# The group norm of the RWKV heads moved into the chunk recurrence, its output gate computed as a weight stage, the merge gates fetched into chunks already read, and splits that cover only a unit's rows

## The chip, the cores and the metric

The kernel runs on one core of a Trainium2 chip. The metric is the device time of one execution in microseconds (us). The kernel before takes 3714.7 us (median of three runs, 3714.55 to 3715.57).

## The reference

The program is a five layer model over 512 tokens of width 1024, in float32. The first four layers (two RG-LRU mixers, a gated spatial mixer, a short convolution, each with an MLP) are touched by the change in one detail only. The fifth layer is where the change sits:

```
rw = shifted projections;  q, k, v, gate_r, gate_a = the rest of n @ w_in
g = sigmoid(p_gd) @ g2                                  # 160 x 1024
y = rwkv7_scan(r, decay, k, v, -kk, kk * a)             # 16 heads of 64, token by token
mean, var over the 64 channels of a head
yn = (y - mean) * rsqrt(var + GN_EPS) * gn_w + gn_b
y_rwkv = (yn + sum(r * k * r_k) * v) * g
merged = sigmoid(gate_r) * (y_rwkv @ p_rwkv) + sigmoid(gate_a) * (y_attn @ p_attn)
h = h + merged @ w_out, then cross attention and an MLP
```

`sum(r * k * r_k) * v` is called the bonus.

## The kernel before, in words

**Layout and weight stages.** Activations lie with channels on the 128 partitions and the 512 tokens along the free axis, so a tensor of width 1024 is 8 tiles of 128x512. Nearly all dense products go through a weight stage. A stage consists of groups, each giving two output tiles, and a group of one or two units. A unit is a block of kb x 128 weight rows by 256 columns. SyncE loads it into one of two slots of `raw` (`sp_stage`, L374), ScalarE copies it to the rounded `wh` (L387), VectorE computes the rest `wl = raw - wh` (L391), and TensorE multiplies three terms (xh*wh, xl*wh, xh*wl, L441) for each 128 rows and each output tile: 6 matmuls for each k, 48 for a unit of 8, 30 for one of 5 (`l0_out` and `l3_out`, two units a group), 12 for one of 2 (`p_attn`). Both copies work on all 8 row blocks of the slot, whatever kb is. The next unit's split stands in each engine's queue ahead of the work on this group's results (`split_next`, L394). Evacuated activations are split in the same way (`act_upper` L776 gives yh, `dve_lower_y` L780 gives yl).

**Order of the fifth layer.** The queues of the engines are written out by hand, in program order: ... `rkv`, `gates2`, then `pe_chunks`, `pe_heads`, the stage `merge`, `out2`. The sigmoids of the 16 merge gate tiles go to DRAM (`gate_spill`) from `tmp` (L1200), the 8 bonus tiles as well (L1449).

**Chunks (L1542 to L1693).** The recurrence runs over 8 chunks of 64 tokens. In a chunk, five levels (l = 1 to 5) of small 64x64 products invert a triangular matrix: `Y` (L1559), then `X` (L1578) and `Z` (L1579), where ScalarE copies Y out and VectorE adds X and Z. W0 is made in levels 2 and 3, then come U (L1586), the new state (L1593, L1595) and the chunk's output (L1599 to L1603), which ScalarE copies into `VT` (L1635). The halves of the partitions (`HP`) hold two heads, and their products alternate. TensorE turns V, B and K of the next chunk by an identity (`i64`, L1534).

**Heads (L1696 to L1757).** After the last chunk GpSimd fetches g2 and the bonus. For each of the 8 tiles TensorE sums over heads (L1702), VectorE centres (L1738), ScalarE squares (L1721), TensorE sums again (L1712), ScalarE takes the root (L1725), VectorE takes the reciprocal of 128x512 (L1747), scales, adds the bonus and multiplies with the gate tile that TensorE made in float32 (L1715, L1716; L1748 to L1752). Splits of the result follow.

**Merge (L1781).** Eight groups alternate between p_rwkv (8 row blocks) and p_attn (2). GpSimd loads all gates with one 4 MB DMA (L1773) and then `x` (L1775).

Of the kernel before, what the change touches and what calls it, by code (L numbers as in the profile page):

```python
# [90 lines left out]
def build(nc, a, out):  # L91
# [39 lines left out]
    i64 = pers("i64", [P, CH])  # L131
    ARENA = used[0] + (WH_AT - used[0]) % 512
# [78 lines left out]
    gl = at("gl", 0, [P, 16, T], base_at=XH_AT)  # L211
    mg = at("mg", 0, [P, ND, T])
    g2s = at("g2s", 0, [P, 2, D])
    gns = at("gns", 8, [P, 3, T])
    bon = at("bon", 14, [P, 2, T])
# [21 lines left out]
    bonus_spill = nc.dram_tensor("bonus_spill", [ND, P, T], F32).ap()  # L237
    kv_spill = nc.dram_tensor("kv_spill", [P, 16, MEM], F32).ap()
# [27 lines left out]
    def stage(name, *args, **kw):  # L266
# [4 lines left out]
        back = {"x": ND, "h": 16, "y": 5 * st.upg if st.upg == 2 else ND + 2 * (name == "merge"), "m": None}[st.rhs]  # L271
# [4 lines left out]
        st.loop = st.kind in ("relu", "resid", "fin", "gelu", "sigm", "scale", "gelusq") and not st.classes  # L276
# [74 lines left out]
    tiles_split("ysplit", ND + 2)  # L351
# [18 lines left out]
    srcs = {"x": (xh, xl), "h": (hh, hl), "y": (yh, yl), "m": (mh, ml)}  # L370
# [3 lines left out]
    def sp_stage(sp, st):  # L374
        def body(p, first):
            for su in range(st.upg):
                w, r, kb, c = weights(st, p.j, su)
                src = w.rearrange("(k p) n -> p k n", p=P)[:, r:r + kb, bass.ds(c, 256)]
                sp.wait_ge(lower, p.unit(su) + 1)
                sp.dma_start(raw[:, p.slot(su), 0:kb], src).then_inc(landed[p.slot(su)], 16)  # L380
        run_groups(sp, st, body)

    def act_split(act, p, su):
# [16 lines left out]
    def pe_stage(pe, st):  # L400
        ops = srcs[st.rhs]
        need = (lambda k: st.need0 + k + 1) if st.need0 is not None else None

        def body(p, first):
            banks = [ps[2 * p.pair()], ps[2 * p.pair() + 1]]
            pe.wait_ge(evac, p.group() * 2 + 2)
            for su in range(st.upg):
                slot = p.slot(su)
                kb = st.kb if st.kind != "merge" else (8, 2)[p.c % 2]
# [17 lines left out]
                for k in range(kb):  # L427
                    kk = k0 + k
                    if st.kind == "merge" and p.c % 2:
                        kk = ND + k  # L430
                    if need and (p.c < 1 or st.kind == "merge"):
                        pe.wait_ge(split, need(kk))
# [6 lines left out]
                    for mt in mts:  # L439
                        for n_, (wt, oi) in enumerate(terms):  # L440
                            last = nc.tensor.matmul(banks[mt][:, 0:st.n], wt[:, slot, k, mt * P:mt * P + P],  # L441
                                                    ops[oi][:, kk, 0:st.n],
# [48 lines left out]
    def act_stage(act, st, dest=None, fn=None, custom=None):  # L491
        def body(p, first):
# [9 lines left out]
            for mt in range(2):  # L502
                t = p.j * 2 + mt
                if custom or st.kind in ("scale", "resid", "conv4", "tok", "memk", "memv"):
# [58 lines left out]
    def dve_stage(dve, st, dest=None, custom=None, early=None):  # L563
        def body(p, first):
            split_next(dve_split, dve, p, st)
            if first:
                dve_norm(dve, st.norm)
                if st.name == "q":
                    dve.wait_ge(s("mid_root"), 1)
                    nc.vector.reciprocal(acc1[:], acc1[:]).then_inc(s("mid_inverted"), 1)  # L570
# [108 lines left out]
    def pe_init(pe):  # L679
# [5 lines left out]
        last.then_inc(s("rows_turned"), 1)  # L685
# [23 lines left out]
    def dve_init(dve):  # L709
        dve.wait_ge(s("rows_turned"), 1)  # L710
# [5 lines left out]
        nc.vector.tensor_scalar(prm[1][:, G_SQ:G_SQ + ND], prm[1][:, G_SQ:G_SQ + ND], EPS, None, ALU.add).then_inc(s("mid_gains"), 1)  # L716
        nc.vector.tensor_scalar(omu[:, 0:27], prm[3][:, MU:MU + 27], -1.0, 1.0, ALU.mult, ALU.add)
        for t in range(ND):
            dve.wait_ge(s("x_turned"), t + 1)
# [5 lines left out]
    def act_init(act):  # L725
# [4 lines left out]
        act.wait_ge(s("mid_gains"), 1)  # L730
# [3 lines left out]
    def dve_softplus(dve):  # L734
# [21 lines left out]
        nc.vector.tensor_copy(small[:, 4:5], q[:, 0:1]).then_inc(s("c8_ready"), 1)  # L756
# [79 lines left out]
    def act_a(act, l):  # L836

        n, j = f"l{l}", l // 3
        for t0 in range(0, NR, 2):
# [5 lines left out]
            if t0 == 0:  # L845
                act.wait_ge(s("c8_ready"), 1)
# [171 lines left out]
    def pool_dist(pool):  # L1018


        pool.wait_ge(s("dist_free"), 1)
# [22 lines left out]
    def dve_x(dve, ts):  # L1044

        dve.wait_ge(s("mid_inverted"), 1)
# [1172 lines left out]
```

## Time and profile before

| | |
|---|---|
| median of three runs | 3714.7 us |
| the profiled execution's own time | 3715.44 us |
| its span in the profile | 3713.7 us |
| mean granted TensorE clock | 0.974 |
| TensorE busy, share of the span | 3553.9 us, 96% |
| VectorE busy | 1871.4 us, 50% |
| ScalarE busy | 1162.3 us, 31% |
| GpSimd busy | 442.4 us, 12% |

Busy time says how long an engine had an instruction in flight. Matmuls overlap (a 128x512 matmul counts 0.39 us and the next one starts 0.23 us later), so the share of TensorE tells of gaps, not of peak speed. The granted clock is the share of TensorE's full 2.4 GHz; 0.5 is its lower level, 1.2 GHz.

### The profile page before, as it was taken

Reading aid. Unit: us, or ns where it says so; the run is one execution under the profiler, and the core shown is the slowest. Engines: PE = TensorE matmul, PEld = TensorE weight load, DVE = VectorE, ACT = ScalarE, POOL = GpSimd, SP = SyncE. Lnnn points to the kernel's source line nnn. Section 1 sums busy time; section 2 is a strip of 40 time slices with the busy share of each in tenths; the row PEclk is TensorE's granted clock in tenths of the full one; section 3 lists DMA queues with packets and bytes.
Section 4 is the critical chain, followed back from the end, with each engine's and each line's share of the span. In section 5 each row is a group of like instructions: output and inputs, shape, how many; then the busy total and the mean of one; then the engine's idle time right before and its main releaser. Section 6 shows DMA issues by size and latency. Waiting matters only on the chain. (4 is left out here: it accounts for less than half of the span.)

```text
span 3713.7 us, 52132 instructions
## 1 busy us (share of the span) xinstructions
PE 3553.9 (96%) x21576; PEld 2877.8 (77%) x21576; DVE 1871.4 (50%) x2099; ACT 1162.3 (31%) x1319; POOL 442.4 (12%) x416
## 2 busy tenths in 40 slices
PE   7999999899999999999999999999999988989998
PEld 5578888778888888887678888887769965768886
DVE  7655244335344553346654344564785556455242
ACT  3632123222222232222632133233652222233122
POOL 1111011011011020111111012000220000112011
PEclk9999999889999999999999999999999989999998
DMA  3123233213223233233123323342220004312331
GB/s 123 60 84 102 94 98 96 68 57 102 91 91 101 91 102 102 91 102 103 50 88 102 98 93 104 105 130 97 89 83 21 4 24 155 101 46 91 102 101 57
DMA packets 296102, 324.80 MB, mean 87 GB/s; under 512 B 5971, under 2 KB 287958, under 8 KB 295415
## 3 DMA queue, kind: packets, MB, share of 16 engines
q1 hardware_dynamic: 288439, 295.92, 25.0%
q0 software_dynamic: 5184, 22.15, 1.7%
q10 hardware_dynamic: 2304, 4.20, 0.3%
q8 instruction: 134, 2.20, 0.3%
q14 instruction: 41, 0.34, 0.0%
HBM read 309.66 MB, written 12.58 MB: 87 GB/s over the span
## 5 line engine op out<-in xcount | busy, mean ns | idle before, releaser
L441 PE MATMUL ps<-xh,wh 128*128 128x512 f32 x2424 | 960.4, 396 | 25.4 <-DVE wl L391 22.0
L441 PE MATMUL ps<-xh,wl 128*128 128x512 f32 x2424 | 947.2, 391 | 0.0
L441 PE MATMUL ps<-xl,wh 128*128 128x512 f32 x2424 | 947.1, 391 | 0.0
L391 DVE TENSOR_TENSOR wl<-raw,wh 128x2048 fp32r<-128x2048 f32 x283 | 656.2, 2319 | 449.2 <-ACT wh L387 448.7
L387 ACT ACTIVATE wh<-raw 128x2048 fp32r<-128x2048 f32 x283 | 540.4, 1910 | 693.3 <-PE ps L441 668.5
L441 PEld LDWEIGHTS ps<-xh,wh 128*128 128x128 f32 x2424 | 457.7, 189 | 135.4 <-issue 36.9
L441 PEld LDWEIGHTS ps<-xl,wh 128*128 128x128 f32 x2424 | 457.9, 189 | 99.7 <-issue 5.8
L441 PEld LDWEIGHTS ps<-xh,wl 128*128 128x128 f32 x2424 | 457.4, 189 | 96.4
L441 PE MATMUL ps<-hh,wh 128*128 128x512 f32 x1280 | 498.3, 389 | 1.1 <-DVE wl L391 0.9
L441 PE MATMUL ps<-hl,wh 128*128 128x512 f32 x1280 | 498.0, 389 | 0.0
L441 PE MATMUL ps<-hh,wl 128*128 128x512 f32 x1280 | 497.9, 389 | 0.0
L542 POOL TENSOR_TENSOR hf<-tmp 128x512 f32<-128x512 f32 x160 | 163.3, 1042 | 1132.4 <-DVE tmp L580 1132.4
L511 ACT ACTIVATE hh<-tmp 128x512 f32 (+1 forms) x160 | 98.0, 634 | 598.6 <-DVE tmp L580 598.6
L441 PEld LDWEIGHTS ps<-hh,wh 128*128 128x128 f32 x1280 | 240.3, 188 | 52.1 <-DVE wl L391 2.4
L441 PEld LDWEIGHTS ps<-hh,wl 128*128 128x128 f32 x1280 | 240.3, 188 | 50.1
L441 PEld LDWEIGHTS ps<-hl,wh 128*128 128x128 f32 x1280 | 240.3, 188 | 49.6
L580 DVE SCALAR_TENSOR_TENSOR tmp<-ps,rs 128x512 f32<-128x512 f32 x160 | 103.1, 686 | 341.1 <-PE ps L441 341.0
L591 DVE TENSOR_TENSOR x<-x,ps 128x512 f32 (+1 forms) x128 | 82.3, 684 | 379.9 <-PE ps L441 379.9
L555 POOL TENSOR_TENSOR acc<-acc,hf 128x512 f32<-128x512 f32 x88 | 130.3, 1481 | 1057.5 <-ACT hf L523 1026.6
L441 PE MATMUL ps<-yh,wh 128*128 128x512 f32 x496 | 199.3, 402 | 29.9 <-DVE wl L391 17.6
L441 PE MATMUL ps<-yl,wh 128*128 128x512 f32 x496 | 197.2, 398 | 0.0
L441 PE MATMUL ps<-yh,wl 128*128 128x512 f32 x496 | 196.9, 397 | 0.0
(390 smaller groups left out, 3593.8 us busy)
## 6 DMA issues: line engine op xcount, KB each, us to landing
raw<-in_mlp_w SPq DMA_DIRECT2D x128, 1024.0 KB, 5.4
raw<-in_ffn_w SPq DMA_DIRECT2D x32, 1024.0 KB, 5.4
raw<-in_w_in SPq DMA_DIRECT2D x31, 1024.0 KB, 5.3
raw<-in_a_w_in SPq DMA_DIRECT2D x20, 1024.0 KB, 5.1
raw<-in_c_w_in SPq DMA_DIRECT2D x12, 1024.0 KB, 5.2
raw<-in_a_w_out SPq DMA_DIRECT2D x16, 640.0 KB, 4.4
raw<-in_b_w_in SPq DMA_DIRECT2D x8, 1024.0 KB, 5.4
raw<-in_xa_wkv SPq DMA_DIRECT2D x8, 1024.0 KB, 5.5
```

The lines of the kernel that those rows point to most:

```text
L387: nc.scalar.activation(wh[:, p.slot(su)], raw[:, p.slot(su)], ACT.Copy).then_inc(upper, 1)
L391: nc.vector.tensor_tensor(wl[:, p.slot(su)], raw[:, p.slot(su)], wh[:, p.slot(su)], ALU.subtract).then_inc(lower, 1)
L441: last = nc.tensor.matmul(banks[mt][:, 0:st.n], wt[:, slot, k, mt * P:mt * P + P], ops[oi][:, kk, 0:st.n], start=k == 0 and su == 0 and n_ ...
L511: nc.scalar.activation(hh[:, bass.ds(t, 1)], tmp[:, mt:mt + 1, 0:T], ACT.Square).then_inc(acted, 1)
L542: nc.gpsimd.tensor_tensor(hf[:, mt], tmp[:, mt, 0:T], tmp[:, mt, 0:T], ALU.mult).then_inc(pooled, 1)
L555: nc.gpsimd.tensor_tensor(acc[:], acc[:], sq[:, mt], ALU.add).then_inc(pooled, 1)
L580: nc.vector.scalar_tensor_tensor(out=tmp[:, mt, 0:T], in0=ps[b + mt][:], scalar=0.0, in1=rs[:], op0=ALU.max, op1=ALU.mult).then_inc(evac, 1)
L591: nc.vector.tensor_tensor(xt, xt, ps[b + mt][:].rearrange("p (a n) -> p a n", a=1), ALU.add).then_inc(evac, 1)
```

## The change

- **Splits of a unit's rows only.** L387 and L391 work on `rows_of(unit)` row blocks (5 in `l0_out` and `l3_out`, 2 for `p_attn` and g2), and stages with kb = 5 are no longer hardware loops.
- **Gate as a stage.** A new stage `g2` of four units (128 + 32 rows, 12 matmuls each) stands between `gates2` and the chunks. gd and the attention output ya are split for it and for the merge (`gdh`, `gdl`, `yah`, `yal`). Its tiles are copied to two holding places and stored in `g_spill`.
- **Norm in the recurrence.** V is turned by `c64` = identity - 1/64, so the chunk outputs are centred already. During chunk c+1 the norm of chunk c is done: squares (ScalarE), sums (8 matmuls, 2 columns each), root of 64x16, reciprocal of 64x16, 16 matmuls that spread the result, one multiply (VectorE), and three operations on GpSimd (gn_w, bonus + gn_b, gate). Bonus and gate slices come from DRAM into the read slices of B and K.
- **Merge.** The four p_attn groups come first, then the four of p_rwkv. Gates are fetched two tiles at a time into the chunk slices that were read.
- Some semaphores share a name now; no wait is changed by that.

```diff
-        st.loop = st.kind in ("relu", "resid", "fin", "gelu", "sigm", "scale", "gelusq") and not st.classes
+        st.loop = st.kind in ("relu", "resid", "fin", "gelu", "sigm", "scale", "gelusq") and not st.classes and st.kb != 5
+    stage("g2", a["g2_2"][0], 4, 1, 2, lin(0), rhs="g", kind="g2")
-            return (a["p_rwkv_2"][0], 0, 8, j // 2 * 256) if j % 2 == 0 else (a["p_attn_2"][0], 0, 2, j // 2 * 256)
+            return (a["p_attn_2"][0], 0, 2, j * 256) if j < 4 else (a["p_rwkv_2"][0], 0, 8, (j - 4) * 256)
...
+                if st.kind == "merge" and p.c == 1:
+                    sp_g(sp)
+                    sp_slices(sp)
...
-        nc.scalar.activation(wh[:, p.slot(su)], raw[:, p.slot(su)], ACT.Copy).then_inc(upper, 1)
+        nc.scalar.activation(wh[:, p.slot(su), 0:n], raw[:, p.slot(su), 0:n], ACT.Copy).then_inc(upper, 1)
-        nc.vector.tensor_tensor(wl[:, p.slot(su)], raw[:, p.slot(su)], wh[:, p.slot(su)],
+        nc.vector.tensor_tensor(wl[:, p.slot(su), 0:n], raw[:, p.slot(su), 0:n], wh[:, p.slot(su), 0:n],
...
+    def dve_g2(p, b):
+        if p.c < 2:
+            for mt in range(2):
+                nc.vector.wait_ge(s(f"gate_stored{mt}"), 128)
+        else:
+            nc.vector.wait_ge(s(f"g_stored{p.c % 2}"), 32)
+        for mt in range(2):
+            nc.vector.tensor_copy(G_HOLD[p.c % 2][mt], ps[b + mt][:]).then_inc(evac, 1)
+        if p.c == 0:
+            for h in range(2):
+                nc.vector.wait_ge(s("side_upper"), h + 3)
+                nc.vector.tensor_tensor(yal[:, h], ya[:, h], yah[:, h], ALU.subtract).then_inc(s("side_split"), 1)
+    def sp_g(sp):
+        for j in range(4):
+            for mt in range(2):
+                sp.wait_ge(evac, (stages["g2"].g0 + j) * 2 + 5 + mt)
+                sp.dma_start(g_spill[2 * j + mt], G_HOLD[j % 2][mt]).then_inc(s(f"g_stored{j % 2}"), 16)
+    def sp_slices(sp):
...
+        for c in range(NC):
+            sp.wait_ge(s("ck_turned"), 3 * c + 3)
+            if c:
+                sp.wait_ge(s("slices"), 32 * c)
+            tok = slice(c * CH, c * CH + CH)
+            sp.dma_start(BT[:, c], bonus_spill.rearrange("q p t -> p q t")[:, :, tok]).then_inc(s("slices"), 16)
+            sp.dma_start(KT[:, c], g_spill.rearrange("q p t -> p q t")[:, :, tok]).then_inc(s("slices"), 16)
...
+                    plink(nc.gpsimd.tensor_scalar(PT[e % 2][4], PT[e % 2][4], col(3, GNB + e), None, ALU.add))
...
+    def pe_head_sums(pe, c):
+        pe.wait_ge(s("hd_squared"), c + 1)
+        for q in range(NH2):
+            last = mm(ps[HB(c)][0:64, 2 * q:2 * q + 2], hs[c][:, q], headones[:, 0:P:64], start=True, stop=True)
+        last.then_inc(s("hd_sums"), 1)
+    def pe_head_spread(pe, c):
+        pe.wait_ge(s("hd_inverse"), c + 1)
+        for q in range(NH2):
+            for e in range(2):
+                last = mm(ps[HB(c)][HP[e], cols(q)], RT[:, 2 * q + e:2 * q + e + 1].to_broadcast([64, CH]), i64[0:64, :],
+                          start=True, stop=True)
+        last.then_inc(s("hd_spread"), 1)
...
@@ pe_chunks, levels
+                    if l == 2 and c:
+                        pe_head_sums(pe, c - 1)
+                if l == 5 and c:
+                    pe.wait_ge(s("ck_w0_copied"), 2 * c + 2)
+                    pe_head_spread(pe, c - 1)
...
@@ end of pe_chunks
         pe.wait_ge(s("ck_state"), NC)
+        pe_head_sums(pe, NC - 1)
+        pe_head_spread(pe, NC - 1)
...
@@ act_chunks, levels
+                if l == 1 and c:
+                    act_head_squares(act, c - 1)
+                if l == 2 and c:
+                    act_head_root(act, c - 1)
...
@@ dve_chunks
+                if l == 3 and c:
+                    dve_head_inverse(dve, c - 1)
+            if c:
+                dve_head_scale(dve, c - 1)
...
     def pool_heads(pool):
+        for c in range(NC):
+            tok = VT[:, :, c * CH:c * CH + CH]
+            pool.wait_ge(s("hd_scaled"), c + 1)
+            pool.wait_ge(s("slices"), 32 * c + 32)
+            plink(nc.gpsimd.tensor_tensor(hs[c][:], hs[c][:], prm[3][:, GNW:GNW + ND].unsqueeze(2).to_broadcast([P, NH2, CH]), ALU.mult))
+            plink(nc.gpsimd.tensor_tensor(hs[c][:], hs[c][:], BT[:, c], ALU.add))
+            nc.gpsimd.tensor_tensor(tok, hs[c][:], KT[:, c], ALU.mult).then_inc(s("ysplit_y"), 1)
...
+            pool.dma_start(gl[:, 2 * c:2 * c + 2], gate_spill[src:src + 2].rearrange("t p n -> p t n"))\
+                .then_inc(s("gates_back_attn" if c < 4 else "gates_back_rwkv"), 16)
...
@@ merge
+    def dve_before_merge(p):
+        if p.j == 3:
+            for t in range(2):
+                dve_lower_y(nc.vector, "ysplit", t, VT[:, t])
+    def act_merge(p):
+        ts = {2: (0, 1), 3: range(2, ND)}.get(p.j, ())
+        for t in ts:
+            act_upper(nc.scalar, "ysplit", t, VT[:, t], src=NC)
```

## Rows read from the trace of the kernel before

**Rows 1.** Timeline of TensorE: start us, duration, instructions, idle time ahead and its releaser.

```profile
214.58 0.80 PE L441 MATMUL ps<-yh,wh 128*128 128x512 f32 x1 [5.21 <-DVE wl L391]
...
232.17 0.50 PE L441 MATMUL ps<-yh,wh 128*128 128x512 f32 x1 [1.14 <-DVE wl L391]
...
2786.22 3.68 PE L1539 MATMUL ps<-AR,BT 64*64 64x128 f32 x32 [7.19 <-DVE small L1645]
...
3026.70 0.28 PE L1603 MATMUL ps<-TLK,cVt 64*64 64x64 f32 x4
...
3090.84 0.80 PE L441 MATMUL ps<-yh,wh 128*128 128x512 f32 x1
...
3158.00 0.77 PE L441 MATMUL ps<-yh,wh 128*128 128x512 f32 x1 [5.02 <-DVE yl L780]
3158.56 0.63 PE L441 MATMUL ps<-yl,wh 128*128 128x512 f32 x1
3158.99 0.63 PE L441 MATMUL ps<-yh,wl 128*128 128x512 f32 x1
```

**Rows 2.** Windows: stretch, length, busy PE, PEld, DVE, ACT, POOL, clock, DMA share, GB/s.

```profile
2786.20:3027.00 240.80, 237.10 (x7168) 229.20 (x7168) 126.95 (x270) 61.55 (x143) 0.15 (x1) 0.99 0.03 9
...
3033.60:3092.00 58.40, 47.35 (x67) 15.33 (x68) 51.52 (x45) 15.43 (x24) 4.94 (x8) 0.73 0.26 82
```

**Rows 3.** VectorE's groups by form, 2200 to 3300 us: busy, mean ns, idle.

```profile
L391 DVE TENSOR_TENSOR wl<-raw,wh 128x2048 fp32r<-128x2048 f32 x63 | 145.7, 2313 | 100.1 <-ACT wh L387 100.1
...
L1747 DVE RECIPROCAL gns<-gns 128x512 f32<-128x512 f32 x8 | 26.8, 3348 | 2.9 <-ACT gns L1725 2.9
...
L1924 DVE COPY qx<-ps 128x512 f32<-128x512 f32 x8 | 5.2, 686 | 20.1 <-PE ps L1899 20.1
```

**Rows 4.** DMA issues: KB each, median us from issue to landing.

```profile
gate_spill<-tmp ACTq DMA_DIRECT2D x16, 256.0 KB, 2.0
raw<-in_p_rwkv SPq DMA_DIRECT2D x4, 1024.0 KB, 5.3
...
x<-x_spill POOLq DMA_DIRECT2D x1, 2048.0 KB, 19.4
```

**Rows 5.** Timelines of ScalarE and VectorE in a chunk: waits after level 1 and level 5.

```profile
2918.50 0.38 ACT L1627 ACTIVATE cYt<-ps 128x256 f32<-128x256 f32 x1 [2.18 <-PE ps L1559]
...
2903.56 1.29 DVE L1651 TENSOR_TENSOR TLB<-ps,acc 128x512 f32<-128x512 f32 x2 [1.33 <-PE ps L1539]
```

**Rows 6.** GpSimd's groups by form.

```profile
L1443 POOL TENSOR_TENSOR KT<-rt 128x512 f32<-128x512 f32 x8 | 10.4, 1297 | 0.0
```

**Rows 7.** Timeline of TensorE in a chunk: level 4 and the start of level 5.

```profile
2925.82 1.37 PE L1559 MATMUL ps<-cX,cTM 64*64 64x64 f32 x32
2927.03 0.63 PE L1578 MATMUL ps<-cYt,cZ 64*64 64x64 f32 x16
...
2928.89 1.37 PE L1559 MATMUL ps<-cX,cTM 64*64 64x64 f32 x32
```

**Rows 8.** Timeline of TensorE around eight tiny matmuls between two weight units.

```profile
2314.27 0.39 PE L441 MATMUL ps<-xl,wh 128*128 128x512 f32 x1
2314.50 0.39 PE L441 MATMUL ps<-xh,wl 128*128 128x512 f32 x1
2314.82 1.05 PE L1064 MATMUL ps<-ones,rs 1*128 1x1 f32 x8
2315.79 0.50 PE L441 MATMUL ps<-xh,wh 128*128 128x512 f32 x1
```

**Rows 9.** Timeline of TensorE in an attention slot: float32, 64 rows, 128 moving columns.

```profile
2493.55 0.38 PE L1097 MATMUL ps<-kT,qT 64*128 64x128 f32 x2
2493.77 0.38 PE L1098 MATMUL ps<-kT,qT 64*128 64x128 f32 x2
```

**Rows 10.** Timelines of ScalarE and VectorE in `l0_out`, ahead of its fourth unit.

```profile
227.74 1.91 ACT L387 ACTIVATE wh<-raw 128x2048 fp32r<-128x2048 f32 x1
...
229.67 2.44 DVE L391 TENSOR_TENSOR wl<-raw,wh 128x2048 fp32r<-128x2048 f32 x1 [0.86 <-ACT wh L387]
```

More of the change, by code:

```diff
@@ L210, in build @@
     tgtf = at("tgtf", 1.25, [P, CH], base_at=XT_AT)
[L211 to L215, printed above, removed]
+    gl = at("gl", 0, [P, 16, T])
+    mg = at("mg", 0, [P, ND, T], base_at=XH_AT)
+    hs = [at(f"hs{c}", 4 * c, [P, NH2, CH]) for c in range(NC)]
+    gdh = at("gdh", 2, [P, 2, T], F32R, base_at=XT_AT)
+    gdl = at("gdl", 84, [P, 2, T], F32R)
+    yah = at("yah", 28, [P, 2, T], F32R, base_at=XH_AT)
+    yal = at("yal", 80, [P, 2, T], F32R)
     qx = at("qx", 0, [P, ND, T])
@@ L366, in weights, with rows_of @@
         if st.kind == "merge":
-            return (a["p_rwkv_2"][0], 0, 8, j // 2 * 256) if j % 2 == 0 else (a["p_attn_2"][0], 0, 2, j // 2 * 256)
+            return (a["p_attn_2"][0], 0, 2, j * 256) if j < 4 else (a["p_rwkv_2"][0], 0, 8, (j - 4) * 256)
         return st.w, st.row0 + su * st.kb, st.kb, st.col(j)
-    srcs = {"x": (xh, xl), "h": (hh, hl), "y": (yh, yl), "m": (mh, ml)}
+    srcs = {"x": (xh, xl), "h": (hh, hl), "y": (yh, yl), "m": (mh, ml), "g": (gdh, gdl)}
+    unit_rows = [8 if st.kind != "merge" and st.kb is None else st.kb if st.kb else (2 if c < 4 else 8)
+                 for st in order for c in range(st.groups) for _ in range(st.upg)]
+    G2_U0 = stages["g2"].u0
+    def rows_of(u):
+        return unit_rows[u] if isinstance(u, int) else 8
     def sp_stage(sp, st):
@@ L684, in pe_init @@
                                        ident[0:n_rows[i], 0:n_rows[i]])
[L685 removed]
+        last.then_inc(s("x_turned"), 1)
         pe.wait_ge(s("x_landed"), 16)
@@ L1200, in act_gates @@
             act.dma_start(gate_spill[p.st.first + t], tmp[:, mt, 0:T]).then_inc(s(f"gate_stored{mt}"), 16)
+        if p.st.name == "gates2" and p.c == 0:
+            act.wait_ge(s("pair_pooled"), 5 * ND - 5)
+            act.wait_ge(s("lora_ready"), 3)
+            for h in range(2):
+                act.activation(gdh[:, h], gd[:, h], ACT.Copy).then_inc(s("side_upper"), 1)
         act_attn_slot(act, k)
@@ L1212, in dve_gates, with act_g2 @@
                 dve_chunk_masks(nc.vector)
+                for h in range(2):
+                    nc.vector.wait_ge(s("side_upper"), h + 1)
+                    nc.vector.tensor_tensor(gdl[:, h], gd[:, h], gdh[:, h], ALU.subtract).then_inc(s("side_split"), 1)
         dve_attn_scores(nc.vector, after_group(p.st, p.c))
+    G_HOLD = [[tmp[:, 0, 0:T], tmp[:, 1, 0:T]], [rs[:], rt[:, 0]]]
+    def dve_g2(p, b):
[6 more added lines that the diff above has]
+            nc.vector.tensor_copy(G_HOLD[p.c % 2][mt], ps[b + mt][:]).then_inc(evac, 1)
+        if p.c == 0:
+            for h in range(2):
+                nc.vector.wait_ge(s("side_upper"), h + 3)
+                nc.vector.tensor_tensor(yal[:, h], ya[:, h], yah[:, h], ALU.subtract).then_inc(s("side_split"), 1)
+    def act_g2(p):
+        if p.c == 0:
+            nc.scalar.wait_ge(units, stages["gates2"].u0 + 4)
+            for h in range(2):
+                nc.scalar.activation(yah[:, h], ya[:, h], ACT.Copy).then_inc(s("side_upper"), 1)
+    def sp_g(sp):
[4 more added lines that the diff above has]
+    def sp_slices(sp):
+        for m in range(2):
+            sp.wait_ge(s(f"bonus_stored{m}"), 64)
+            sp.wait_ge(s(f"g_stored{m}"), 64)
+        for c in range(NC):
[5 more added lines that the diff above has]
+            sp.dma_start(KT[:, c], g_spill.rearrange("q p t -> p q t")[:, :, tok]).then_inc(s("slices"), 16)
     def shift_scale(p, mts, mu, dests):
@@ L1718, in act_heads @@
-    def act_heads(act):
-        def root(q):
-            act.wait_ge(s("hd_centred"), q + 1)
-            act.activation(gns[:, 2], VT[:, q], ACT.Square).then_inc(s("hd_squared"), 1)
-            act.wait_ge(s("hd_var"), q + 1)
-            if q >= 2:
-                act.wait_ge(s("ysplit_y"), q - 1)
-            act.activation(gns[:, q % 2], ps[5][:], ACT.Sqrt, scale=1.0 / 64, bias=small[:, 1:2]).then_inc(s("hd_root"), 1)
-        root(0)
-        for q in range(ND):
-            if q + 1 < ND:
-                root(q + 1)
-            act_upper(act, "ysplit", q, VT[:, q])
-        for h in range(2):
-            act.activation(yh[:, ND + h], ya[:, h], ACT.Copy).then_inc(acted, 1)
@@ L1825, in act_mem_norm @@
             act.wait_ge(s("mem_summed"), c + 1)
-        act.activation(msq[:, 2:4], msq[:, 0:2], ACT.Sqrt, scale=1.0 / D, bias=small[:, 0:1]).then_inc(s("mem_root"), 1)
+        act.activation(msq[:, 2:4], msq[:, 0:2], ACT.Sqrt, scale=1.0 / D, bias=small[:, 0:1]).then_inc(s("mem_summed"), 1)
     MEM_TILES = (0, 2, 4, 6, 1, 3, 5, 7)
```

180 lines of the change are left out of this document (91 added, 89 removed).

## The prediction

> **What bounds the kernel now.** I read the page first: TensorE is in flight 96% of the span (the table above), so only two things can move the time, its own work and its gaps. Then I listed the gaps from its timeline [rows 1]: between the end of `gates2` and the start of `out2` stands the largest cluster of the kernel, and `l0_out` and `l3_out` show four each that end with a weight split (5.21 us once, and then three like the one of 1.14). The windows [rows 2] say what each stretch is made of. In the chunks (240.8 us) TensorE is busy 237.1 us at a granted clock of 0.99: that stage is bound by TensorE. In the heads stage VectorE is busy 51.5 of 58.4 us, and TensorE's clock is 0.73: that stage is bound by VectorE, above all by eight reciprocals of 3.35 us [rows 3]. The merge is bound by TensorE again.
>
> The stations of TensorE before, from [rows 1]: `gates2` ends at 2786.2 - 7.2 = 2779.0; the chunks run from 2786.2 to 3027.0; the merge starts at 3090.8; `out2` starts at 3158.0. I predict the last station, then add `l0_out` and `l3_out`.
>
> **The g2 stage, up to the chunks.** On TensorE it is 4 x 12 matmuls, 0.227 us apart when the clock is up (the pair that shows it stands further down), 10.9 us. VectorE, which today is late already (it releases the chunks 7.2 us after TensorE is free), gets more: 8 copies of PSUM by 0.686 [rows 3] = 5.5; four subtractions for gd and ya, of the same 512 columns and as long, 2.7; five splits of 2 row blocks by some 0.7 in place of one of 2.3, +1.2; one small operation, 0.2. That is 9.6. To this come waits that the new order makes: the first copy needs the last gate tile stored (2.0 us after its issue [rows 4]), and the third needs the first g tiles stored, whose DMA stands in SyncE's queue behind the load of merge unit 0, which waits for the split of g2 unit 2. Followed instruction by instruction, the copies of group 2 start at about 2794.3, those of group 3 at 2796.7, and the chunks at 2798.9: **+12.7 us**. Bounds: 8.5 (VectorE's work less what it waits through today) and 18 (each of the two holding places waits a store and its queue in full).
>
> **In the chunks, seven times.** ScalarE's squares (some 0.6) fall behind its Y copies of level 1, where it then waits 2.2 us; root and reciprocal are 64x16 and small; VectorE's multiply (0.69) falls into 1.3 us that it waits for the B products [rows 5]; GpSimd's three operations (1.3 each [rows 6], some 4.5 with their links) have a chunk of 29 us. If these covers were gone, a chunk would be 0.6 to 0.7 us longer for each. TensorE has no cover: a level is 96 instructions in 3.07 us, 2.80 us of them issue at 29 ns [rows 7], so what is added to it lies on the path. A float32 matmul is two instructions. Sums: 16 instructions, each with 64 weight columns and 2 moving. The nearest rows are eight instructions with 128 weight columns and one moving, 0.97 us, 0.12 each [rows 8]; half the columns give some 0.06, so 1.0 us. Leaving the 64x64 pattern and coming back costs some: that same break starts 0.09 us later than the pitch would have it [rows 8]; I take 0.3 with the semaphore. Bounds 0.5 (29 ns each) and 1.9 (0.12 each). Spread: 32 instructions, 64 weight columns, 64 moving. All read the lower 64 partitions, so they can't alternate between halves as the pairs at 29 ns do. Two instructions with 64 rows and 128 moving columns take 0.22 us [rows 9], 0.11 each, so 64 columns take 0.055: 1.7 us. Bounds 0.9 (as pairs) and 3.4 (0.107 each, load and multiply one after the other). The spread stands where TensorE waits 0.25 us for the last Y copy, which it fills. Sum 1.3 + 1.7 - 0.25 = 2.75, times seven **+19.3 us** (8 to 36).
>
> The Trainium skill says (TensorE: Matmul & The Clock Gate, The mechanism) that a weight load overlaps a running matmul only when the row group differs. By that rule the spread would cost 3.4 us and the sum 12 us more. The trace disagrees where it can be seen: matmuls that all use the full array, each with its own weights, start 0.227 us apart, which is little more than 512 columns take [rows 8], and the instructions of [rows 9], all on the same 64 rows, come no slower than their moving columns ask for.
>
> **After the chunks.** Let T be the end of the last chunk, 2798.9 + 240.8 + 19.3 = 3059.0. The last norm has no cover: output copy and squares until T+1.5, sums T+2.8, root and reciprocal T+3.9, spread T+6.0 or somewhat more at the lower clock. The merge starts at T+6.5, where before it started 63.8 us after the chunks: **-57.3 us**. The heads stage is gone, since the reciprocals of 512 columns became ones of 16 and the rest went to GpSimd.
>
> **Merge to out2.** The matmuls are the same 240, 54.4 us. Before, the stretch took 67.2 us, with gaps for a split of 2.3 us behind an evacuation between the units, and 5.0 at its end [rows 1]. Now the four short units come first. They finish by T+19.5, and the first p_rwkv unit is late: its load waits for the split of p_attn unit 2 (T+11.5), takes 5.3 us alone [rows 4] and more beside the gates and `x` (2 MB), which GpSimd issues at about T+13, so it lands at T+18.5; ScalarE +1.9, VectorE +2.3, the lower part of y tile 0 +0.7: TensorE starts at T+23.7, with a clock that has to come up (1.9 us: after 5 us of idling, nine matmuls stood 0.43 apart, not 0.227 [rows 1]). Four units of 10.9 us then run without a gap, to T+69.2. The next stage's split is no longer in front of the last evacuation, so `out2` starts 2.8 + 0.7 us later, T+72.5. From merge start that is 66.0: **-1.2 us**. GpSimd's last three operations (done by T+12.5) hide behind the short units. If that cover were gone, `out2` would move with them.
>
> Sum of the layer: 12.7 + 19.3 - 57.3 - 1.2 = **-26.5 us**; `out2` starts at 3131.5.
>
> **Splits of five row blocks.** In `l0_out` the fourth unit's split runs 1.91 on ScalarE and 2.44 on VectorE, one after the other behind the evacuation, and TensorE waits 1.14 for it [rows 1, 10]. With 5/8 of the columns they take 1.2 and 1.45, 1.7 us less in all, so the gap goes. The first matmul behind the gap is 0.1 to 0.2 us longer too, so I take 1.3 for each. The first gap (5.21) shrinks by ScalarE 0.7 and VectorE 0.85, 1.5. 1.5 + 3 x 1.3 = 5.4 for each stage, **-11 us** for both. Bounds: 8 (the first gap stays) and 13 (it shrinks by the whole 1.7 and the clock comes up sooner). Splits of other stages are untouched.
>
> Total -37.5, against the profiled execution's own 3715.4 (0.7 above the median): 3677.9, or **3677 us** beside the median.
>
> **Rivals.**
> 1. The spread's loads are not hidden. For it: nothing in this kernel alternates two column halves over the same 64 rows. Against: [rows 9]. Worth 1.7 x 7 = 12: 3689 us. It is what the rule of the Trainium skill above would give.
> 2. The transfers crowd: gates, `x` and the weights of two p_rwkv units meet at T+13, and `x` took 19.4 us beside the 4 MB gate load [rows 4]. Each us that unit lands later is a us; with the g2 stage at its upper bound too (stores waited in full), 3 to 10 us: 3684.
> 3. Cheaper small work: sums and spread issue at 29 ns as the pairs do, and g2 is at its lower bound. 19.3 becomes 8, 12.7 becomes 9: 3662 us.
> 4. Row splits don't bite, because another queue holds those units (the activation's own split, ScalarE's wait for the multiply before). Then -3 in place of -11: 3685.
> 5. Slower than before. Sums are a full-height pattern in a stream of 64x64 ones, and every change of pattern might drain the array. There are 14 changes, two for each of seven chunks; they undo the gain of 37.5 us only above 2.7 us each, and then 3715 and beyond. Against: the break in [rows 8] starts 0.09 us late. The Trainium skill (TensorEngine Tiling (Array Packing), Key Properties) does say that switching the tiling mode drains TensorE, but gives no price; [rows 8] show one that is small.
>
> **How the numbers follow.** Forecast 0.50, with its own range 3668 to 3686; rival 1 0.15; rival 2 0.12; rival 3 0.12; rival 4 0.04; rival 5 0.04 for its full form and 0.03 for a weak one that ends within 0.2% of no change. 0.2% is 7.4 us, about what a measurement of this kernel can tell from no change. Faster 0.93, same 0.03, slower 0.04. The range that leaves out no more than 2 in 10 reaches from the middle of rival 3 and its half above, 3661, to beyond rival 1, 3696.
>
> **What would show it.** In the profile after: the first chunk product 20 us after `gates2`; 27 to 28 us of further chunk time against 240.8 would speak for rival 1, 19 for the forecast, 8 for rival 3; the clock in the chunks stays at 0.99; no reciprocal of 128x512 after the chunks; one gap of some 4 us before the first p_rwkv unit and none between units; periods of 13.6 us in `l0_out`. It would be wrong if the chunk levels start to wait on ScalarE or VectorE, or if the clock falls in the chunks.

## The result, and the profile after

The changed kernel takes 3677.8 us (median of 4 runs, 3676.4 to 3684.7), the one before 3714.8 us; the ratio is 0.990, 95% interval 0.989 to 0.992. The prediction was 3677 us. The profiled execution's own time is 3676.4 us, its span 3674.2 us.

Timeline of TensorE of the changed kernel at its stations (columns as in [rows 1]):

```profile
211.97 0.79 PE L476 MATMUL ps<-yh,wh 128*128 128x512 f32 x1 [3.77 <-DVE wl L417]
...
2768.29 0.76 PE L476 MATMUL ps<-gdh,wh 128*128 128x512 f32 x1 [4.45 <-DVE wl L417]
...
2784.76 3.61 PE L1625 MATMUL ps<-AR,BT 64*64 64x128 f32 x32 [2.19 <-DVE small L1786]
...
3040.67 0.28 PE L1735 MATMUL ps<-TLK,cVt 64*64 64x64 f32 x4
3042.59 1.06 PE L1637 MATMUL ps<-headones,hs 128*64 128x2 f32 x16 [1.63 <-DVE cST L1838]
3044.29 1.97 PE L1645 MATMUL ps<-i,small 64*64 64x64 f32 x32 [0.64 <-DVE small L1659]
3046.20 0.79 PE L476 MATMUL ps<-yah,wh 128*128 128x512 f32 x1
...
3068.84 0.77 PE L476 MATMUL ps<-yh,wh 128*128 128x512 f32 x1 [9.21 <-DVE yl L815]
...
3119.01 0.54 PE L476 MATMUL ps<-yh,wh 128*128 128x512 f32 x1 [3.53 <-DVE yl L815]
```

Against [rows 1]: `gates2` ends at 2763.8 (idle time of 4.45 ahead of 2768.29), where it ended at 2779.0. The chunks follow 20.9 us later instead of 7.2. The last chunk ends at 3041.0 (its last row starts at 3040.67). The merge starts 5.2 us after that instead of 63.8. Of the four idle times in `l0_out`, the first fell from 5.21 to 3.77 and the three of 1.14 are gone. A gap of 9.2 us stands ahead of the first p_rwkv unit, and none between units.

Windows of the changed kernel: g2, chunks, last norm, p_attn groups, the gap, p_rwkv groups (columns as in [rows 2]).

```profile
2763.80:2784.80 21.00, 14.17 (x51) 9.11 (x50) 15.84 (x32) 4.72 (x8) 2.15 (x2) 0.92 0.41 150
2784.80:3041.00 256.20, 250.79 (x7504) 242.76 (x7504) 139.22 (x284) 68.34 (x158) 32.28 (x28) 0.99 0.14 36
3041.00:3046.20 5.20, 2.97 (x49) 2.80 (x49) 1.62 (x3) 2.02 (x4) 0.00 (x0) 0.80 0.29 99
3046.20:3059.60 13.40, 13.40 (x50) 10.55 (x48) 6.35 (x10) 2.31 (x4) 5.28 (x5) 0.82 0.57 209
3059.60:3068.80 9.20, 0.03 (x1) 0.00 (x0) 3.00 (x3) 4.95 (x8) 0.00 (x0) 0.77 0.71 237
3068.80:3119.00 50.20, 46.64 (x192) 38.04 (x193) 25.55 (x31) 11.13 (x12) 0.44 (x1) 0.94 0.32 105
```

The chunk stage has 336 instructions more (7 x 48) and is 15.4 us longer than in [rows 2]. TensorE is still busy for nearly all of it, with the clock at 0.99. In the gap TensorE has nothing, the DMA engines are at 0.71, and 237 GB/s is the highest rate of these windows. That what TensorE waits for there is a transfer is shown by ScalarE's row under runs 3 and 4.

Timeline of VectorE of the changed kernel in the g2 stage, at its longest wait:

```profile
2780.95 1.29 DVE L1269 COPY tmp<-ps 128x512 f32<-128x512 f32 x2 [3.02 <-DMA g_spill<-tmp]
```

The copy of g2's third group waits 3.0 us for the first g tiles to be stored, which is the wait that the prediction put there.

Timeline of TensorE in the chunk that [rows 5] and [rows 7] show: sums in level 2, and the spread of the chunk before.

```profile
2904.44 1.04 PE L1645 MATMUL ps<-i,small 64*64 64x64 f32 x30
2905.27 0.27 PE L1709 MATMUL ps<-cZ,cYt 64*64 64x64 f32 x1
2905.32 0.22 PE L1645 MATMUL ps<-i,small 64*64 64x64 f32 x1
2905.37 1.04 PE L1709 MATMUL ps<-cZ,cYt 64*64 64x64 f32 x30
...
2925.41 1.09 PE L1637 MATMUL ps<-headones,hs 128*64 128x2 f32 x16
2926.43 0.68 PE L1708 MATMUL ps<-cYt,cZ 64*64 64x64 f32 x16
```

The x30 of the spread start at 2904.44 and the next product's x30 at 2905.37: 32 instructions in 0.93 us, 29 ns each, the pitch of the pairs in [rows 7]. The 16 of the sums take 1.02, 64 ns each.

The chunks are not all alike. From its first product to that of the next, each of the second to the seventh takes 29.66 to 29.83 us in the kernel before. In the changed kernel three of them take 31.47 to 31.59 and the other three 32.09 to 32.34. In the long ones TensorE stops for a moment in the middle of a level, and the profile names no engine for it:

```profile
2891.86 0.50 PE L1682 MATMUL ps<-cX,cTM 64*64 64x64 f32 x9 [0.54 <-issue]
```

There are four such breaks, 1.4 us in all. The kernel before has none.

### The profile page after: what moved, and what is told of

The parts are those of the page before. It is cut to its first block and busy times, and to the rows that moved or that the text cites. A ratio compares the mean times of both kernels' runs of the same rounds, so it can differ in the third digit from the quotient of the medians.

```text
span 3674.2 us, 52665 instructions
## 1 busy us (share of the span) xinstructions
PE 3536.7 (96%) x21944; PEld 2888.8 (79%) x21944; DVE 1827.8 (50%) x2090; ACT 1145.6 (31%) x1325; POOL 490.6 (13%) x445
## 5 line engine op out<-in xcount | busy, mean ns | idle before, releaser
L417 DVE TENSOR_TENSOR wl<-raw,wh 128x2048 fp32r<-128x2048 f32 (+2 forms) x287 | 642.6, 2240 | 457.4 <-ACT wh L412 456.8
L412 ACT ACTIVATE wh<-raw 128x2048 fp32r<-128x2048 f32 (+2 forms) x287 | 527.1, 1837 | 712.3 <-PE ps L476 678.2
L476 PE MATMUL ps<-yh,wh 128*128 128x512 f32 x480 | 192.0, 400 | 22.4 <-DVE yl L815 12.7
```

The lines of the kernel that those rows point to most:

```text
L412: nc.scalar.activation(wh[:, p.slot(su), 0:n], raw[:, p.slot(su), 0:n], ACT.Copy).then_inc(upper, 1)
L417: nc.vector.tensor_tensor(wl[:, p.slot(su), 0:n], raw[:, p.slot(su), 0:n], wh[:, p.slot(su), 0:n], ALU.subtract).then_inc(lower, 1)
L476: last = nc.tensor.matmul(banks[mt][:, 0:st.n], wt[at_, slot, k, mt * P:mt * P + P], ops[oi][at_, kk, 0:st.n], start=k == 0 and su == 0 an ...
```

## The experiments

Each was timed beside the kernel before (3714.6 to 3715.9 us). Medians are of 4 executions where nothing else is said. Single executions of one kernel scatter by up to 11 us here (run 7), so each verdict goes by the median and by the stations of the trace together. T is the end of the last chunk, and "after T" counts from there. For each run the diff shows its main lines; "..." stands for lines left out.

**1. Rows undone.** The changed kernel, with eight row blocks split in `l0_out` and `l3_out`.

```diff
-        return unit_rows[u] if isinstance(u, int) else 8
+        return unit_rows[u] if isinstance(u, int) and unit_rows[u] != 5 else 8
```

> The changed kernel with one part undone: the splits of the two stages with five row blocks (l0_out and l3_out) work on all eight row blocks again; these stages stay written out and everything else stays as changed. From the two traces, the changed kernel's TensorE is 6.6 us ahead before the end of layer 0 and 15.2 us ahead at the end of gates2. If the shorter splits made all of that, this kernel takes 3677.8 + 15 = 3693 us. If my working holds (5.4 us a stage) and the rest comes from elsewhere, 3689. Rival: writing the loops out instead of running them as hardware loops made the gain, not the rows; then this kernel stays at 3678 to 3682, and the gaps before the fourth and later units of l0_out stay closed.

Measured: 3685.3 us, 7.5 above the changed kernel. That fits neither theory and not the rival in full: part of the gain stays with eight row blocks.

**2. Loops out, in the kernel before.** The other half: only the loop flag of the change.

```diff
-... "gelusq") and not st.classes
+... "gelusq") and not st.classes and st.kb != 5
```

> The kernel before with one line of the change alone: the stages with five row blocks (l0_out, l3_out) are written out instead of running as hardware loops; the splits still work on eight row blocks. In the run with the rows undone and the loops out, the gaps before the later units of l0_out were 0.57 us where the kernel before has 1.14, and the units came 14.5 us apart instead of 15.0 to 15.1; its TensorE was 5.8 us ahead of the kernel before at g2, where the changed kernel is 15.2 ahead. Theory: writing the loops out is worth 5 to 6 us by itself, 3709.3; the rows are the other 9.4. Rival: the loops cost nothing, the 5.8 us came from elsewhere in the change (semaphores that share a name, placement), and this kernel stays at 3714.8.

Measured: 3708.2 us (10 executions, 3706.2 to 3710.7), 6.5 less than before; ratio 0.998 (0.997 to 0.999, which is 3 to 10 us). Timeline of TensorE in `l0_out` of this kernel:

```profile
229.96 0.50 PE L441 MATMUL ps<-yh,wh 128*128 128x512 f32 x1 [0.58 <-DVE wl L391]
...
244.42 0.50 PE L441 MATMUL ps<-yh,wh 128*128 128x512 f32 x1 [0.56 <-DVE wl L391]
```

The groups come 14.46 us apart, and each gap is half of the 1.14 of [rows 1]; the trace still names the split as what ended it. So of each gap half was the hardware loop's and half the split's. From the first product of `l0_out` to the first of the next stage, and the same for `l3_out`, TensorE takes 133.8 us in the kernel before, 129.0 in this one and 122.4 in the changed one. So in the traces the loops are worth 4.8 us (3.8 of it in the six gaps) and the rows 6.6, together 11.4 for both stages. The medians say 6.5 and 7.5; the traces don't show the difference in these stages.

**3 and 4. Transfers held.** In run 3 GpSimd's load of x waits until ScalarE has split the first p_rwkv unit. In run 4 the last gates and the second p_rwkv load wait for that too (the second and third piece below).

```diff
         pool.wait_ge(s("x_stored"), 16)
+        pool.wait_ge(upper, stages["merge"].u0 + 5)
         pool.dma_start(x[:], x_spill)
...
+            if c == NC - 1:
+                pool.wait_ge(upper, stages["merge"].u0 + 5)
             pool.wait_ge(s("ysplit_y"), c + 1)
...
+                if st.kind == "merge" and p.c == 5:
+                    sp.wait_ge(upper, p.unit(su))
```

> The changed kernel with one transfer moved: GpSimd issues the 2 MB load of x only after ScalarE has split the first p_rwkv unit. Theory (transfers crowd): the first p_rwkv load took 10.4 us instead of 5.3 because x, issued 1.1 us before it, shares the DMA engines; a quarter MB of gates and the second p_rwkv load still share. I expect a landing 6.5 us after the issue, the gap before the first p_rwkv unit 9.2 - 4 = 5.2 us, and 3674 us. Rival: the time is that of SyncE's own queue, where the loads of units 4 and 5 share the engines; then the gap stays at 9 us and the time at 3678. A second way to fail: x is then late for the last stage of the layer and out2 waits for it.

> As the run before, and two more transfers are held: the last pair of gates (0.5 MB) also waits until the first p_rwkv unit is split, and SyncE's load of the second p_rwkv unit waits until then too. The first p_rwkv load then has the engines for itself. Theory (transfers crowd): landing 5.3 us after the issue as in the kernel before, gap 4.1 us, out2 5 us earlier than in the changed kernel, 3673 us. Against the run before it tells what the second load and the gates cost: 1.2 us by this theory, nothing if x alone was the crowd. Rival: the load is slow by itself here (gap stays 9 us, 3678).

Measured: 3675.6 and 3670.6 us, 2.2 and 7.2 below the changed kernel. Timelines of SyncE's queue and ScalarE: changed kernel, x later, all held, in this order.

```profile
3053.38 15.10 SPq L401 DMA_DIRECT2D raw<-in_p_rwkv  x3
...
3063.85 1.91 ACT L412 ACTIVATE wh<-raw 128x2048 fp32r<-128x2048 f32 x1 [7.90 <-DMA raw<-in_p_rwkv]
```

```profile
3060.01 11.96 SPq L401 DMA_DIRECT2D raw<-in_p_rwkv  x3
...
3067.34 1.91 ACT L412 ACTIVATE wh<-raw 128x2048 fp32r<-128x2048 f32 x1 [4.79 <-DMA raw<-in_p_rwkv]
```

```profile
3061.27 9.56 SPq L403 DMA_DIRECT2D raw<-in_p_rwkv  x3
...
3066.20 1.92 ACT L414 ACTIVATE wh<-raw 128x2048 fp32r<-128x2048 f32 x1 [2.36 <-DMA raw<-in_p_rwkv]
...
3071.18 0.47 PE L478 MATMUL ps<-yh,wh 128*128 128x512 f32 x1 [3.68 <-DVE yl L817]
```

From issue to the split's start it is 10.5, 7.3 and 4.9 us, and the gap is 9.2, 6.1 and 3.7 us. The load is slowed by all that runs beside it: x is worth 3 us of the gap, gates and second load together 2.4. `out2` starts 78.0, 74.4 and 69.8 us after T. Holding x cost nothing later: from `out2` to the end it is 555 us in all three. Both profiled executions are the slowest of their four; ahead of T, the stretch from `gates2` to the chunks took 4.8 and 7.2 us longer in them than in the changed kernel (see runs 11 and 12).

**5. Spread twice.** In the seven covered chunks.

```diff
-        for q in range(NH2):
+        for q in list(range(NH2)) * (2 if c < NC - 1 else 1):
             for e in range(2):
```

> The changed kernel in which TensorE computes the spread of the head norm twice (same values into the same bank) in each of the seven chunks that run under the next one: 32 more instructions a chunk. If they cost 29 ns each, as the row of the changed kernel says (x30 in 0.9 us), the seven add 6.5 us: 3684.3. By my forecast's price (0.055 us each) 12.3 us: 3690. If a weight load waits for the running matmul of the same 64 rows (0.107 us each), 24 us: 3702. The second copy has no wait to fill, so this is the bare price.

Measured: 3681.7 us, 3.9 more. The stretch from the first to the last chunk is 6.3 us longer, 0.9 us a chunk for 32 instructions, 28 ns each. This settles the price: rows 7, not rows 9.

**6. Sums in two places.**

```diff
+                if l == 2 and c:
+                    pe.wait_ge(s("ck_out"), c)
+                    pe_head_sums(pe, c - 1, range(0, 4))
...
-                        pe_head_sums(pe, c - 1)
+                        pe_head_sums(pe, c - 1, range(4, NH2))
```

> The changed kernel with the eight head sums of a chunk in two places, four before and four after the first W0 products of level 2, in the seven chunks that run under the next one: the same instructions, but two more changes of pattern (64x64 to full height and back) in each of seven chunks. If a change of pattern costs what the changed kernel's rows show (some 0.1 to 0.2 us a break), the time rises by 1 us, within what a measurement can tell. If changes of pattern drain the array at more than 2.7 us each, as rival 5 had it, it rises by 38 us. The first half also has to wait for ScalarE's squares one place earlier; 0.5 us a chunk if they are late.

Measured: 3683.1 us (one execution 3676.2). In the trace the chunks start 6.7 us later than in the changed kernel, where the two are alike; 4.8 of that is the g2 stage, with the clock at 0.66. The chunks themselves are 0.8 us longer. Their breaks without a releaser are shorter here (0.8 us in all, not 1.4), so without them the difference is 1.4 us, some 0.1 us for each of the 14 more changes of pattern. Chunks without a break say the same: 31.7 to 31.8 us instead of 31.5. A change of pattern has a price, but it is far from rival 5's 2.7 us.

**7. GpSimd's work out.** One column in place of the three operations, in seven chunks.

```diff
+            if c < NC - 1:
+                nc.gpsimd.tensor_tensor(VT[:, 0, c * CH:c * CH + 1], hs[c][:, 0, 0:1], KT[:, c, 0, 0:1], ALU.mult).then_inc(s("ysplit_y"), 1)
+            else:
...
```

> Leaves out: GpSimd's three operations (gn_w, bonus, gate) of the first seven chunks, for each of which one single-column product stands; the last chunk is whole. It prices what GpSimd's work costs the recurrence that it lies under. In the changed kernel two of VectorE's operations on SBUF took 0.98 and 1.71 us for the pair instead of 0.69 and 0.76 while GpSimd worked, and TensorE shows a new gap of 0.39 us behind them. Theory: contention costs 0.4 us a chunk, 3675 us. Rival: TensorE is the bound of the chunk and hides it, 3678 us (no change). A third: the rest of the added chunk time (2.2 us a chunk, of which sums and spread are 2.0) is all matmuls, which says the same as the rival.

Measured: 3680.6 us (3674.6 to 3685.5), the chunks as long as in the changed kernel (within 0.1 us). VectorE's groups in the chunks, of the changed kernel and of this one (columns as in [rows 3]):

```profile
L1807 DVE TENSOR_TENSOR cZ<-cTM,i 128x256 f32<-128x256 f32 x16 | 11.8, 776 | 0.3
...
L1803 DVE TENSOR_TENSOR cTM<-TLB,acc 128x512 f32<-128x512 f32 x8 | 7.2, 906 | 0.3
```

```profile
L1807 DVE TENSOR_TENSOR cZ<-cTM,i 128x256 f32<-128x256 f32 x16 | 6.1, 422 | 0.3
...
L1803 DVE TENSOR_TENSOR cTM<-TLB,acc 128x512 f32<-128x512 f32 x8 | 5.5, 692 | 0.3
```

The contention is real, 7.4 us of VectorE's time in all, and hidden: VectorE waits later in the chunk for TensorE anyway, 12.1 us in all before it updates the state and 19.5 without GpSimd's work. The rival holds.

**8. Another order around g2.** gd's subtractions ahead of the chunk masks, the masks in three parts, the first two g stores ahead of the load of merge unit 0.

```diff
         if p.c == 0:
-            dve_chunk_masks(nc.vector)
...
+            dve_chunk_masks(nc.vector, 0)
...
     def dve_g2(p, b):
+        if p.c in (0, 2):
+            dve_chunk_masks(nc.vector, 1 + p.c // 2)
...
+                if st.kind == "merge" and p.c == 0:
+                    sp_g(sp, (0,))
```

> The changed kernel with the work around g2 in another order, nothing left out: VectorE's subtractions for gd stand ahead of the chunk masks, the masks are built in three parts (before the last evacuation of gates2, and in the two places where the copies of g2 wait for a store), and SyncE issues the first two g stores ahead of the load of merge unit 0. Theory: the idle time of 4.45 us before g2 and the 3.0 us wait for the store are what the chunks start late by, and the idle time is also what lets TensorE's granted clock fall to 1.2 GHz: in one profiled execution of the kernel with all transfers held the clock stood at 0.50 from 2775 to 2785 us and the chunks came 23.6 us after the first g2 matmul instead of 16.5. With the idle time short the clock should stay up: the chunks start 4 us earlier than in the changed kernel (17 us after gates2), 3674 us, and no execution lies 7 to 8 us above the others. Rival: VectorE's own work (some 22 us of it) sets the start of the chunks in whatever order, then the time stays within 1 us of 3678 and the slow executions stay too.

Measured: 3682.1 us, a miss. g2 now starts without a gap, but the chunks come 21.9 us after `gates2`, not 20.9, and gaps of 1.8 us stand between the g2 groups. Timeline of VectorE behind the third of these groups:

```profile
2785.90 1.26 DVE L1590 TENSOR_TENSOR acc<-acc 128x64 f32<-128x64 f32 x5 [3.12 <-PE ps L478]
```

Where VectorE waited 3.0 us for a store, it now waits 3.1 us for TensorE, whose clock was at 0.77 in this stage and whose work there took 2.3 us longer. So the order moved the wait and did not remove it. The rival's cause, VectorE's own work, is not shown apart from this clock. The rest of the 4.3 us arose before the end of `gates2`, where the trace is 5.4 us behind that of the changed kernel.

**9 and 10. Together.** Transfers held as in run 4, and the first p_attn group right behind the last output. Run 9 has the order of run 8, run 10 only its earlier store.

```diff
         pe.wait_ge(s("ck_out"), NC)
+        pe_stage(pe, stages["merge"], (0,))
         pe.wait_ge(s("ck_state"), NC)
         pe_head_sums(pe, NC - 1)
...
         act_head_squares(act, NC - 1)
+        act_split(act, At(stages["merge"], 0, 0, 0), 1)
         act_head_root(act, NC - 1)
...
+        dve_split(dve, At(stages["merge"], 0, 0, 0), 1)
         dve_head_inverse(dve, NC - 1)
...
-        ts = {2: (0, 1), 3: range(2, ND)}.get(p.j, ())
+        ts = {2: range(5), 3: range(5, ND)}.get(p.j, ())
```

> The changed kernel with the order around g2 of the run before, all three transfers held as in the third run, and the first p_attn group moved: TensorE multiplies it right behind the last chunk's output, ahead of the last head sums, where it waited 1.6 us for ScalarE; the second unit's split stands ahead of the last root and reciprocal; tiles 0 to 3 of y are split ahead of the first p_rwkv unit's weights. Theory: each part gives back its own wait, -4 us (order around g2), -7 us (transfers held, measured 3670.6 against 3677.8), -3 us (first group's 5.1 us at the lower clock leave the path, but the load of the first p_rwkv unit comes only some 3 us earlier): 3664 us. Rival: the last norm's chain gets later by the moved group, y comes later than the weights and the gap before the first p_rwkv unit stays at 5 us or grows; then 3668 or more.

> As the run with all parts together, but with the chunk masks back in their old place (the order around g2 as in the changed kernel, except that the first g stores are issued ahead of the load of merge unit 0). In that run the stretch from the end of gates2 to the chunks took 24.5 us, with the clock down, against 20.9 in the changed kernel; the stretch from the last chunk to out2 took 68.7 against 78.0. Theory: the new order cost 3.6 us through the clock and the rest gained 9.3: 3677.8 - 9.3 - up to 2 (store earlier) = 3667, with single executions 7 us above. Rival: the fall of the clock has nothing to do with the masks and stays: 3670 to 3674.

Measured: 3670.1 and 3670.3 us (3667.0 to 3672.1). `out2` starts 68.7 and 68.8 us after T, where holding alone gave 69.8: the moved group is worth 1 us more, not 3. The first p_rwkv load waits for the split of the third p_attn unit and came only 1.9 us earlier, and four tiles of y ahead of its weights on VectorE gave 1.2 of that away. The earlier store brought nothing (in run 10 the chunks start 20.8 us after `gates2`). In the profiled execution of run 9 that stretch took 24.5 us with the clock at 0.65, but its median is no higher, so run 8's order isn't shown to cost anything by the clock. The theory of run 10 named this cost, and it did not come true.

**11 and 12. Filling.** 20 matmuls that nobody reads ahead of g2, alone (11) and with run 10 and 13 more ahead of the first p_rwkv unit (12).

```diff
+            for _ in range(20 if st.kind == "g2" and p.c == 0 else 13 if st.kind == "merge" and p.c == 4 else 0):
+                nc.tensor.matmul(ps[6][:, 0:P], headones[:], ones[:], start=True, stop=True)
```

> The changed kernel with 20 matmuls more on TensorE (float32, 128 moving columns, some 0.22 us each by the nearest row), into a bank that nobody reads, right ahead of the first g2 matmul, where it waits 4.45 us for VectorE. Nothing is left out. Two of the profiled executions (transfers held, x later) had the clock at 1.2 GHz through the g2 stage, and the executions of the changed kernel lie at 3676 to 3678 and once at 3684.7. Theory: the idle time lets the clock fall, and whether it comes back inside the stage differs from execution to execution; with TensorE kept at work it stays up, the first g2 group takes 2.8 us instead of 5.1 and all executions lie together: 3676.5, none above 3680. Rival: the clock falls through the stage itself (its 32 row matmuls), as in all four executions of the reordered g2 stage, and filling the gap doesn't help: then single executions stay 7 us above the others, or all of them, 3684.

> As the run before, with the 20 filling matmuls ahead of g2 and 13 ahead of the first p_rwkv unit, where TensorE waits 3.3 us and then starts 9 to 10 matmuls at the lower clock (0.43 us apart instead of 0.227). Theory: both starts at the lower clock go (2 us each) and no execution is above the others: 3664 us. Rival: the fillers delay the units behind them or do not hold the clock: 3667 or more.

Measured: 3674.3 us (3673.4 to 3678.5) and **3663.9 us** (3662.8 to 3666.0), ratio to the kernel before 0.987 (0.985 to 0.988), 14 us less than the changed kernel. Windows of the g2 stage, from its first matmul to the chunks: changed kernel, all held, filler alone (columns as in [rows 2]).

```profile
2768.30:2784.80 16.50, 14.13 (x50) 9.07 (x50) 11.68 (x19) 4.72 (x8) 2.15 (x2) 0.91 0.53 191
```

```profile
2769.00:2792.70 23.70, 21.61 (x50) 13.73 (x50) 11.86 (x19) 4.82 (x8) 2.15 (x2) 0.57 0.37 133
```

```profile
2769.30:2785.70 16.40, 12.86 (x49) 8.29 (x48) 11.84 (x19) 4.72 (x8) 2.14 (x2) 1.00 0.53 191
```

The stage with the same 48 matmuls took 7.2 us more in one execution than in another, with the clock at 0.57 instead of 0.91. In the filled one it stood at 1.00, and the chunks still start no earlier (20.8 us after `gates2`): TensorE instead waits 1.3 us between the first two groups, until VectorE's split is done. The 3.5 us of the median are thus not gained there in this trace; 1.4 of them are in the chunks, which have one break without a releaser instead of four. At best the filler keeps a late clock from costing something, and not for certain: in run 12 the clock was at 0.90 in this stage, since it fell for 3 us behind a wait of 1.3 us, and the chunks came 22.0 us after `gates2`. One execution of run 11 also lies 4 us above the others. Ahead of the first p_rwkv unit it does buy: `out2` starts 65.9 us after T instead of 68.8. The medians of runs 10 and 12 are 6.4 us apart, their profiled executions 2.7. Of that, 2.9 are seen behind T, where the unit starts at the full clock and with a gap of 0.4 us, and 1.9 in the chunks, which again have one break (0.3 us) where run 10 has four (1.6); the g2 stage gave 1.3 back, and stages with the same code make up the rest. Why the breaks are fewer with the filling matmuls, and how much of the 6.4 is scatter, stays open.

## Why the prediction was right, and where only its sum was

| step | predicted | measured |
|---|---|---|
| g2 stage up to the chunks | +12.7 | +13.7 |
| chunks, seven times | +19.3 | +15.4 |
| heads tail | -57.3 | -58.6 |
| merge to `out2` | -1.2 | +5.6 |
| up to the end of `gates2` | -11 | -15.2 |
| behind `out2` | 0 | -0.5 |
| sum | -37.5 | -39.5 (spans) |

**Right in mechanism, and close in size where the gain is.** The heads stage is gone: no reciprocal of 128x512 stands behind the chunks and the last norm takes 5.2 us. The cause and, within 1 us, the price of the later chunk start hold in the profiled execution: VectorE's queue with a wait of 3.0 us for the g store. What the prediction did not have is that this stage costs 5 to 7 us more in some executions, with the clock at 0.57 to 0.66. The covers in the chunks hold: run 7 shows it for GpSimd's work, and for ScalarE's and VectorE's the trace does, where TensorE's idle time with a named releaser is 1.9 us in the whole stage, 1.7 before. The clock stayed at 0.99.

**The spread was mis-sized.** The prediction took 1.7 us a chunk from [rows 9], because all its instructions read the lower 64 partitions. It is 0.93 by the rows and 0.9 by run 5. Products that write alternate column halves go at the pitch of the pairs, and that they share their rows costs nothing. Rival 1, and with it the rule of the Trainium skill (TensorE: Matmul & The Clock Gate, The mechanism) that loads overlap only when the row group differs, would have given 3.4; the trace disagrees. The sums were 1.02 and some 0.1 ahead of them, where 1.0 and 0.3 were taken. With 0.93 for the spread the prediction's own sum gives 1.3 + 0.93 - 0.25 = 2.0 a chunk, 13.9 in all; chunks without a break are 1.8 us longer than before. The rest of the 15.4 are the four breaks that name no releaser, 1.4 us by themselves. The prediction had no term for them, and it stays open what makes them: they stand within about 1 us at the same places, 107, 133, 172 and 236 us behind the start of the chunks, in runs 1, 3, 4, 9 and 10, and only one, at another place, is left where the filling matmuls stand ahead (runs 11 and 12).

**The first p_rwkv load was mis-sized, by rival 2's mechanism.** The prediction let it land 7 us after its issue, at T+18.5; it took 10.5, and the issue came 0.9 us later too. Gates, x and the next unit's load share the engines (runs 3 and 4 take it apart). The first p_rwkv unit started at T+27.8 instead of T+23.7, and 14 matmuls at the lower clock followed, some 2.9 us of loss instead of the 1.9 taken. `out2` started at T+78.0 instead of T+72.5. The list of the rival was right, its chance too small: gates, x, this load and the next one were issued within 4.6 us (T+10.5 to T+15.1).

**The splits of five row blocks: the row splits are worth less, and a line that was costed at nothing makes up for it.** The two stages became 11.4 us shorter, as good as the 11 of the prediction, but by luck. The step "1.7 us less in all, so the gap goes" took the whole 1.14 us for the split's. Half of each gap belonged to the hardware loop (run 2). Rows alone are worth 6.6 us by the traces and 7.5 by medians, not 11, and the written out loops 4.8 and 6.5, not 0. With the loop and without it the trace names the split as what released the gap; the releaser named what came last, not what made it late.

**What cancelled.** The prediction had the merge 6.8 us and the g2 stage 1.0 too cheap; chunks, tail and the early stages 3.9, 1.3 and 4.2 too dear. That the total came within 1 us of the median is luck by that much. Of the 15.2 us at the end of `gates2`, 11.4 lie in `l0_out` and `l3_out` and 3.8 in stages whose code is the same. That is what such stages scatter by: two profiled executions that run nearly the same code up to there (runs 1 and 2) are 3.2 us apart at that point, and the last 182 us ahead of it took up to 185 us in other runs of the changed kernel's code.

## What to carry to other kernels

When a stage that was hidden behind a long one is exposed, look at every transfer that starts within a few us of the first load it needs, and hold back those that are needed later: three waits on other transfers were worth 7 us here. Price small matmuls by the nearest row with the same output pattern, and test by doing them twice. Where an edit changes a loop's form along with its work, cost the form by itself, since a gap whose releaser is a split may be half the loop's.

## What was not expected of the hardware

- Hardware loops cost some 0.57 us per group of two units on the critical path in `l0_out` (1.14 to 0.57 us of idle time, runs 1 and 2), without any row that names them.
- TensorE's instruction stream breaks off for 0.2 to 1.3 us in the chunks of the changed kernel and its variants, 0.3 to 3.0 us in all, with no releaser in the trace; the kernel before has no such break there.
- The granted clock of the same short stage was 0.91, 0.65 and 0.57 in three executions that do the same up to there (the changed kernel, runs 3 and 4), and the stage took 16.5, 21.3 and 23.6 us. Of eight profiled executions with this order and no filling, five were at 0.91 and three below 0.67. Behind an idle time of 4.45 us it came back after 6 matmuls, 2.8 us, in one and hardly at all in another. With filling matmuls it was 1.00 and 0.90. What decides it stays open.
- GpSimd's products slow VectorE's that read SBUF alone: 422 to 776 ns for 256 columns, 692 to 906 for 512; those of 512 columns that read PSUM beside GpSimd's (L1792) stayed at 0.68 us.
